# First u product from unnormed x, with the inverse root applied as it is evicted

## What is computed

```
def rmsnorm(x, w):
    y = xf * lax.rsqrt(jnp.mean(xf * xf, axis=-1, keepdims=True) + EPS)
    return (y * w.astype(jnp.float32)).astype(x.dtype)
...
    h = rmsnorm(x, norm1_w)
    proj = h @ w_in
    y_b, s5_new = s5_mixer(proj[..., OFF_U:OFF_Q], ...)
    gates = jax.nn.sigmoid(proj[..., OFF_GATE:].astype(jnp.float32))
```

## Time and profile before

| | |
|---|---|
| median of 3 runs | 1686.33 us |
| profiled execution, span | 1684.5 us |
| TensorE busy | 1654.0 us, 98% |
| VectorE, ScalarE, GpSimd busy | 57%, 33%, 47% |
| first u matmul starts | 17.30 us |
| first tap matmul (needs W) starts | 77.89 us |

### The profile page before, as it was taken

The page is one execution under the profiler, slowest core; times in us unless marked ns, Lnnn a source line. Parts: engine busy times, 40 slices in busy tenths (PEclk is TensorE's granted clock), DMA queues, the critical chain, the costliest instruction groups (busy, mean ns, idle before and its releaser), DMA issues. The chain is left out here.

```text
span 1684.5 us, 30884 instructions
## 1 busy us (share of the span) xinstructions
PE 1654.0 (98%) x12241; PEld 1604.7 (95%) x12241; DVE 966.9 (57%) x1642; ACT 556.0 (33%) x1240; POOL 791.2 (47%) x756
## 2 busy tenths in 40 slices
PE   7999999999999999999999999999999999999997
PEld 7999999999999998888899999999999999999997
DVE  6859811406634554778873289666665565744346
ACT  5332121342213332543411154443443333322233
POOL 5483122322221111141322325877777777787774
PEclk9999999999999999999999999999999999999998
DMA  5364363232233234434365431543433344966443
GB/s 209 84 127 133 104 203 98 89 92 91 87 93 103 89 130 134 161 115 140 126 218 191 152 126 42 180 162 145 151 141 141 141 167 165 367 224 267 162 187 103
DMA packets 95805, 245.85 MB, mean 146 GB/s; under 512 B 14369, under 2 KB 42273, under 8 KB 95417
## 3 DMA queue, kind: packets, MB, share of 16 engines
q1 hardware_dynamic: 73824, 174.48, 30.5%
q0 software_dynamic: 10256, 33.59, 6.7%
q10 hardware_dynamic: 11592, 35.96, 6.3%
HBM read 177.11 MB, written 66.65 MB: 145 GB/s over the span
## 5 line engine op out<-in xcount | busy, mean ns | idle before, releaser
L1642 PE MATMUL ps<-HL,WH 128*128 128x384 f32 (+1 forms) x1536 | 507.7, 331 | 4.4 <-DVE HL L691 1.8
L1643 PE MATMUL ps<-HH,WL 128*128 128x384 f32 (+1 forms) x1536 | 497.4, 324 | 0.0
L1644 PE MATMUL ps<-HH,WH 128*128 128x384 f32 (+1 forms) x1536 | 496.3, 323 | 0.0
L1642 PEld LDWEIGHTS ps<-HL,WH 128*128 128x128 f32 x1536 | 289.4, 188 | 15.6 <-issue 9.3
L1643 PEld LDWEIGHTS ps<-HH,WL 128*128 128x128 f32 x1536 | 289.7, 189 | 0.3
L1644 PEld LDWEIGHTS ps<-HH,WH 128*128 128x128 f32 x1536 | 289.6, 189 | 0.0
L1285 POOL TENSOR_TENSOR WL<-WRAW,WH 128x1024 fp32r<-128x1024 f32 x59 | 145.0, 2457 | 243.3 <-DMA WH<-in_w 243.3
L1282 POOL DMA_DIRECT2D WH<-in_w x59 | 34.6, 586 | 354.4 <-PE ps L1644 352.9
L2932 DVE TENSOR_TENSOR X<-X,ps 128x528 f32<-128x528 f32 (+2 forms) x170 | 107.9, 656 | 155.5 <-PE ps L2238 104.6
L2327 ACT ACTIVATE GT<-ps 128x384 f32<-128x384 f32 (+1 forms) x72 | 33.4, 465 | 215.5 <-PE ps L1644 183.5
L2932 DVE TENSOR_TENSOR RB<-RB,ps 128x528 f32<-128x528 f32 x60 | 42.1, 701 | 103.4 <-ACT RB L2847 85.9
(11 more groups left out here) (467 smaller groups left out, 4266.2 us busy)
## 6 DMA issues: line engine op xcount, KB each, us to landing
WRAW<-in_w SPq DMA_DIRECT2D x75, 512.0 KB, 3.4
ffn_scratch<-STG SPq DMA_DIRECT2D x70, 528.0 KB, 3.6
WH<-in_w POOLq DMA_DIRECT2D x62, 512.0 KB, 4.6
SOP<-ffn_scratch SPq DMA_DIRECT2D x36, 528.0 KB, 7.9
gate_scratch<-GT ACTq DMA_DIRECT2D x24, 528.0 KB, 3.2
PX<-gate_scratch ACTq DMA_DIRECT2D x22, 528.0 KB, 4.2
...
```

Of the source, the lines that this page charges most:

```text
L1642: nc.tensor.matmul(out, wh, rl, start=start, stop=False)
L1643: nc.tensor.matmul(out, wl, rh, start=False, stop=False)
L1644: return nc.tensor.matmul(out, wh, rh, start=False, stop=stop)
```

## The change

The first 384 tokens' u is made from x times the norm weight, without the inverse root; the root is spread into GT and multiplied in when VectorE evicts u (`evict_first_u_dve`). HH and HL of chunk 0 first hold that unnormed x, and are filled again with the normed h for the gates, last of the three chunks (`SPLIT_ORDER`). The roots are taken in the order chunk 1, 0, 2 (`ROOT_ORDER`). The squares of chunk 0 move behind the casts on ScalarE, and GpSimd adds them. The low halves of units 0, 1 and 3 move from GpSimd to VectorE. Units 0 and 1 are loaded as four half tiles issued by ScalarE, and SyncE's queue loads units 2 and 3 right behind chunk 0 of x.

```diff
--- before.py
+++ after.py
...
+    ROOT_ORDER = (1, 0, 2)
+    SPLIT_ORDER = (1, 2, 0)
+    Y_SQUARES, Y_ADDED = 3 * KD, 8
+    SQ0 = UF[:].rearrange("p a t -> p (a t)")[:, 0:KD * 384].rearrange("p (k c) -> p k c", c=384)
...
+        if n == 0:
+            return SQ0[:, k, :]
+        return SQ[:, k if k < 4 else 2 + k % 2, 0:CHUNKS[n][1]]
...
+    def x_plain_high_act(k):
+
+        nc.scalar.wait_ge(s_x[k], 16)
+        if k == 0:
+            nc.scalar.wait_ge(s_par, 16)
+        nc.scalar.mul(HH[:, k, 0:384], X0[:, k, 0:384], prm("norm1", k, 1)).then_inc(xp_hi, 1)
+
+    def x_plain_low_dve(k):
+
+        dve = nc.vector
+        dve.wait_ge(xp_hi, k + 1)
+        dve.scalar_tensor_tensor(HL[:, k, 0:384], X0[:, k, 0:384], prm("norm1", k, 1), HH[:, k, 0:384].bitcast(F32),
+                                 ALU.mult, ALU.subtract).then_inc(xp_lo, 1)
+
+    def x_first_squares_act(ks):
+
+        for k in ks:
+            nc.scalar.activation(SQ0[:, k, :], X0[:, k, 0:384], ACT.Square).then_inc(pq_done, 1)
+
+    def x_first_add_pool():
+
+        pool = nc.gpsimd
+        pool.wait_ge(pq_done, KD)
+        pool.tensor_tensor(SQ0[:, 0:4], SQ0[:, 0:4], SQ0[:, 4:8], ALU.add).then_inc(x0_add, 1)
+        pool.wait_ge(x0_add, 1)
+        pool.tensor_tensor(SQ0[:, 0:2], SQ0[:, 0:2], SQ0[:, 2:4], ALU.add).then_inc(x0_add, 1)
+        pool.wait_ge(x0_add, 2)
+        pool.tensor_tensor(ACC[:, 0:384], SQ0[:, 0], SQ0[:, 1], ALU.add).then_inc(x0_add, 1)
...
     def x_squares_act(n, ks):
         c0, w = CHUNKS[n]
-        base = FIRST_ADDED + KD * (n - 1)
+        added = 4 * (n - 1)
         for k in ks:
-            nc.scalar.wait_ge(x_loaded(n, k), (16, 64, 128)[n])
-            if k >= 4 or n == 2:
-                nc.scalar.wait_ge(pq_used, base + k - 3)
+            nc.scalar.wait_ge(x_loaded(n, k), 128)
+            if k >= 4:
+                nc.scalar.wait_ge(pq_used, added + (1 if k < 6 else 2))
+            elif n == 2:
+                nc.scalar.wait_ge(pq_used, added)
             nc.scalar.activation(x_square_at(n, k), X0[:, k, c0:c0 + w], ACT.Square).then_inc(pq_done, 1)
...
+    def x_add_dve(n, i):
...
+        added, squares = 4 * (n - 1), KD * n
+        if i < 3:
+            dve.wait_ge(pq_done, squares + 4 + 2 * i)
+        if i >= 1:
+            dve.wait_ge(pq_used, added + i)
+        if i < 3:
+            dve.tensor_tensor(SQ[:, 0:2, 0:w], SQ[:, 0:2, 0:w], SQ[:, 2:4, 0:w], ALU.add).then_inc(pq_used, 1)
+        else:
+            dve.tensor_tensor(ACC[:, c0:c0 + w], SQ[:, 0, 0:w], SQ[:, 1, 0:w], ALU.add).then_inc(pq_used, 1)
 
     def x_sums_pe(n):
-        nc.tensor.wait_ge(pq_used, FIRST_ADDED + KD * n)
+        if n == 0:
+            nc.tensor.wait_ge(x0_add, 3)
+            nc.tensor.wait_ge(acc_free[1], 1)
+        else:
+            nc.tensor.wait_ge(pq_used, 4 * n)
+        if n == 2:
+            nc.tensor.wait_ge(acc_free[1], 2)
...
+    def x_root_copy_dve():
+
+        nc.vector.wait_ge(pn_rs, 2)
+        nc.vector.tensor_copy(GT[:, 0:384], x_spread_at(0)[:, 0:384]).then_inc(r0_ok, 1)
+
+    def evict_first_u_dve(j):
+
+        dve = nc.vector
+        dve.wait_ge(r0_ok, 1)
+        dve.wait_ge(acc_done[0], j + 1)
+        dve.tensor_tensor(as_steps(UF[:, j, :], 0, 3), as_blocks(u_bank(j, 0), 3), as_blocks(GT[:, 0:384], 3),
+                          ALU.mult).then_inc(acc_free[0], 1)
...
+            if n == 0:
+                dve.wait_ge(r0_ok, 1)
+                dve.wait_ge(acc_done[0], 4)
+            else:
+                dve.wait_ge(pn_rs, ROOT_ORDER.index(n) + 1)
             if i >= 2:
                 dve.wait_ge(h_lo, i - 1)
-            dve.scalar_tensor_tensor(x_full(i)[:, 0:w], X0[:, k, c0:c0 + w], prm("norm1", k, 1), x_spread_at(n)[:, 0:w],
+            dve.scalar_tensor_tensor(HF[i % 2][:, 0:w], X0[:, k, c0:c0 + w], prm("norm1", k, 1), x_root_spread(n),
                                      ALU.mult, ALU.mult).then_inc(hf_done, 1)
...
         x_chunk(0)
+        first_weights(2)
+        first_weights(3)
+        x_chunk(1)
         sp.dma_start(HOT[:], io["hot"]).then_inc(s_hot, 16)
         sp.dma_start(RTAB[:], io["rtab"]).then_inc(s_hot, 16)
-        first_weights(0)
-        first_weights(1)
-        first_weights(2)
-        x_chunk(1, range(4))
-        x_chunk(1, range(4, KD))
-        first_weights(3)
         x_chunk(2)
...
+        def first_low_third():
+
+            pool.wait_ge(half_ok, 4)
+            pool.sem_inc(split_ok, 2)
+            pool.wait_ge(first_high, 5)
+            pool.wait_ge(s_rawx[0], 16)
+            wh, wl = high_low(2)
+            nc.gpsimd.tensor_tensor(wl, WXR[:, 0, :], wh.bitcast(F32), ALU.subtract).then_inc(split_ok, 1)
+            pool.wait_ge(split_ok, 3)
+            pool.wait_ge(half_ok, 5)
+            pool.sem_inc(split_ok, 1)
...
         s5_angles()
-        split_halves()
-        u = 2
+        first_low_third()
+        x_first_add_pool()
+        s5_powers()
+        s5_rows()
+        u = 4
         while u < FFN + 2:
             need = [None if v < 2 else TILE_END[v - 2] for v in range(UNITS)]
             apart = (*range(6), UNIT0["up0"], UNIT0["up0"] + 1)
@@ -1524,9 +1546,6 @@
             if u in apart:
                 split_apart(u)
                 u += 1
-                if u == 4:
-                    s5_powers()
-                    s5_rows()
...
             if n == 0 and j == 2:
-                pe.wait_ge(split_ok, 4)
+                pe.wait_ge(half_ok, 5)
+                pe.wait_ge(split_ok, 3)
+            elif n == 1 and j == 0:
+                pe.wait_ge(bias_ev, 2)
+            elif n == 1 and j == 2:
+                pe.wait_ge(h_lo, KD)
             elif n == 2:
                 pe.wait_ge(acc_free[0], j + 3 if j == 0 else 4)
                 if j == 2:
-                    pe.wait_ge(acc_free[1], 1)
-            elif n == 1 and j == 2:
-                pe.wait_ge(acc_free[0], 1)
-                pe.wait_ge(h_lo, 2 * KD)
+                    pe.wait_ge(r0_ok, 1)
             for k in range(KD):
                 if j == 0:
-                    pe.wait_ge(h_lo, KD * n + k + 1)
+                    pe.wait_ge(*((xp_lo, k + 1) if n == 0 else (h_lo, KD * (n - 1) + k + 1)))
...
         pe.wait_ge(s_par, 16)
-        x_first_sums_pe()
-        bias_by_distance(0)
-        bias_by_distance(1)
-        x_spread_pe(0)
         u_pair(0, 0)
-        pe.wait_ge(bias_ev, 2)
-        u_pair(2, 0, {1: lambda: x_sums_pe(1), 3: lambda: x_spread_pe(1)})
+        u_pair(2, 0, {3: lambda: x_sums_pe(1), 4: lambda: bias_by_distance(0), 5: lambda: bias_by_distance(1),
+                      6: lambda: x_spread_pe(1)})
         u_pair(0, 1)
-        u_pair(2, 1, {1: lambda: x_sums_pe(2), 3: lambda: x_spread_pe(2)})
+        u_pair(2, 1, {1: lambda: x_sums_pe(0), 3: lambda: x_spread_pe(0), 4: lambda: x_sums_pe(2),
+                      6: lambda: x_spread_pe(2)})
         u_pair(0, 2)
         u_pair(2, 2)
...
         pe.wait_ge(acc_free[1], 4)
-        gate(0, [0, 1])
+        gate(0, [0], lambda n, k: pe.wait_ge(h_lo, 2 * KD + k + 1))
+        gate(0, [1])
...
         act.dma_start(PRM[:, 0:NPAR_FIRST], io["params"][:, 0:NPAR_FIRST]).then_inc(s_par, 16)
+        for half in range(2):
+            c = slice(512 * half, 512 * half + 512)
+            for u in range(2):
+                act.dma_start(WRAW[:, u, c], io["w"][u][:, c]).then_inc(s_half0 if half == 0 else s_raw[u], 16)
...
-        for k in range(0, KD, 2):
-            x_first_square(act, k)
-        nc.scalar.activation(SF("unused_root")[:, 0:1], ZERO[:], ACT.Sqrt)
+        x_plain_high_act(0)
         high_half(0)
-        x_root_act(0)
+        for k in range(1, 4):
+            x_plain_high_act(k)
         high_half(1)
-        x_split_act(0, 2)
-        x_squares_act(1, range(2))
-        x_split_act(2, 3)
-        high_weights(2)
-        x_split_act(3, 4)
-        x_squares_act(1, range(2, 4))
-        x_split_act(4, 5)
-        high_weights(3)
-        x_split_act(5, 6)
-        bias_rows(0)
-        x_split_act(6, 7)
-        bias_rows(1)
-        x_split_act(7, 8)
-        x_squares_act(1, range(4, KD))
-        x_root_act(1)
+        for k in range(4, KD):
+            x_plain_high_act(k)
+        act.wait_ge(ar_ok, 1)
+        nc.scalar.activation(SF("mag"), SF("ar"), ACT.Exp).then_inc(mag_ok, 1)
         act.wait_ge(red_ok, 1)
         nc.scalar.activation(SF("sin"), SF("r"), ACT.Sin)
         nc.scalar.activation(SF("cos"), SF("r2"), ACT.Sin).then_inc(sin_ok, 1)
-        x_squares_act(2, range(4))
-        x_split_act(8, 11)
-        evict_u(0, 0)
-        x_split_act(11, 13)
-        evict_u(1, 0)
-        x_split_act(13, 16)
-        x_squares_act(2, range(4, KD))
-        evict_u(2, 0)
-        evict_u(3, 0)
-        x_root_act(2)
+        high_weights(2)
+        high_weights(3)
+        x_first_squares_act(range(KD))
+        nc.scalar.activation(SF("unused_root")[:, 0:1], ZERO[:], ACT.Sqrt)
+        x_squares_act(1, range(KD))
```

(101 more changed lines are left out.)

93 lines of the change are left out of this document (25 added, 68 removed).

## The result

The changed kernel takes 1712.73 us (median of 4 runs, 1710.41 to 1714.2), the kernel before, timed beside it, 1686.03 us. The ratio is 1.0158, 95% interval 1.0144 to 1.0173. The forecast was 1704.5 with a range of 1696 to 1711: slower was right, the size was 8 us too small and just outside the range. The span of the profiled execution went from 1684.5 to 1709.9 us, 25.4 us more, where the sum had given 18.2.

A forecast was written before the change was run, and what follows sets the result against it. TensorE, busy 1654.0 of 1684.5 us, was taken as the bound, with W setting the first tap. The tap moves from 77.89 to 96.1, 18.2 us later, so 1686.33 + 18.2 = 1704.5 us, range 1696 to 1711.

The forecast's parts named there:

- The place that decides: First tap matmul, at 77.89 us before: it waits for W, which VectorE begins when the last split of h ends.
- Start of TensorE: First u matmul: forecast at 8.6 us instead of 17.30, 8.7 us gained (bounds 7.1 and 10.1).
- Low halves of units 2 and 3: Weights for pair (2,0): ready at 17.6 and 18.8 us, just in time for the first pair's end at 18.8.
- Chunk 1's sums: TensorE's sums of chunk 1's squares: start at 29.7 us, because the squares are late, after a 6.6 us stall.
- the turns of GpSimd and VectorE: Adds of squares: the two engines block each other on a shared port pair; sums at 29.7 us, without it 28.5.
- After the stall: Sums, k-steps, bias products and spread behind the first stall: slow clock costs 1.9 us (bounds 0 and 1.9), spread ends 37.0.
- W: VectorE's six operations ahead of the taps: begin at 78.1 us instead of 59.84, take 17.9, end at 96.0.
- gate 0's stall: TensorE's wait for unit 4's low half (82.4 us): gate 0 done by 92.7, so covered by the wait for W.
- The clock at the taps: Slow clock at the taps after 3.4 us idle: taken at nothing (bounds 0 and 1.9).
- A: Rival: no stall in the u part, W takes 13.7 us without turns, taps 2.0 us earlier: 1684 us; chance 0.06.
- B: Rival: no stall in the u part, but W takes 17.9 us: +2.2 us, 1688.5; chance 0.06.
- C: Rival: half the stalls, chunk 1's sums at about 24 us, splits 5.5 earlier: +8 to 12 us, 1694 to 1698; chance 0.10.

The follow-up runs named there:

- thin_late_split: Changed kernel with the eight normed splits of chunk 0 done over 8 of 384 columns only (measurement only, output not the reference's): 1708.01 us, ratio 1.0128.
- chunk1_first: Changed kernel with ScalarE's squares of chunk 1 ahead of and between those of chunk 0, table load behind all: 1702.03 us, ratio 1.0101.
- warm_first: Changed kernel with 34 unused products on TensorE ahead of chunk 1's sums, to keep it busy in its first stall: 1707.68 us, ratio 1.0122.
- gate_weights: Changed kernel with the casts of weight units 4 and 5 eight splits earlier on ScalarE: 1713.49 us, ratio 1.0162.
- warm_late: Changed kernel with unused products on TensorE, 30 ahead of gate 0's wait and 24 ahead of the first tap: 1711.48 us, ratio 1.0149.

## Why the prediction was wrong

**The place that decides** was read rightly: W behind the last split. thin_late_split and chunk1_first moved W, and the first tap went with it, and nothing behind 145 us gave anything back.

**Start of TensorE**: 8.6 forecast, 8.81 measured. **Low halves of units 2 and 3**: "just in time" was a wait of 0.2 us. **Chunk 1's sums**: 29.7 forecast, 29.34 measured, after 5.8 us idle (6.6 forecast). The list of ScalarE and the turns of GpSimd and VectorE on the squares came out as worked (VectorE's four adds end at 24.2, 26.7, 28.7 and 29.3, forecast 24.3, 27.0, 29.0 and 29.6); chunk1_first, which takes both away, shows that together they were the cause.

**After the stall: the step that failed.** The prediction took 1.9 us for the clock, with bounds 0 and 1.9, from the loss in the first pair before. Measured with and without the slow clock it is 4.45 to the start of the spread and 5.1 to its end. The bound was no bound: it came from a place where nothing but u matmuls followed, and here sums, two bias products, the spread and three k-steps between them followed, all of them at 1.2 GHz from 29.3 to 42.3. The same stretch at the full clock took 5.3 us in warm_first where 4.65 had been reckoned (0.8 + 3.15 + 0.7), 0.65 more. The spread ended at 40.6 instead of 37.0: 3.2 us from the clock (5.1 instead of 1.9) and 0.65 from these products, less 0.4 by which the sums came early. The first matmul of pair (0,1) stood at 42.81 instead of 38.8, and W at 82.38 instead of 78.1. So 3.5 of W's 4.3 us were there at the end of the spread and went through the splits undiminished, as the chain of the prediction has them; 0.7 more came in the splits.

**W**: 17.9 us with two turns, as forecast; gate 0's stall covered, as forecast (gate_weights). The first tap came 4.3 us later than forecast, as much as W began later.

**The clock at the taps** was the second miss: taken at nothing, it was 3.1 us in the profile (44.61 us from tap to STT, 41.46 in warm_late). The argument that 3.4 us of idle time are "nearer to the 2.1 us waits" did not hold: the granted clock is 0.55 behind the 3.07 us. With 5.1 and 3.1 in place of 1.9 and 0 the sum would have been 1710.8. The Trainium skill (TensorE: Matmul & The Clock Gate, on HAM oscillation) has an array that waits between two pieces of work start the next one at half clock. The granted 0.55 behind both stalls agrees, and the sum should have carried the cost at both places.

**The rivals**: A and B needed no stall at all, and the stall was there. C is what chunk1_first makes, but the span is 14.6 us longer there, not 8 to 12. The 8.7 us gained at the start (8.5 measured) are gone as worked, in the late root of chunk 1 and the pairs held to the pace of their splits; the eight splits between chunk 2's and W come on top.

**The range**: its upper end takes 2.7 us for late halves, where landing at 8 instead of 6.4 gives 1.6, and it leaves out half of C and not most of it. Of the 1.9 us between the 1710.8 above and the 1712.73 measured, 1.0 came ahead of W, in the products behind the sums and in the splits, and 1.0 is the distance of the median from the span, 2.8 us instead of 1.8.
